# HGRN's cross products and head outputs regrouped by pairs and heads, and its softplus and scans spread over weight pieces

## The reference, cut to what matters

```python
    z = to_heads(f_logit.astype(f32), HGRN_HEADS)
    logf = jnp.logaddexp(jnp.log(lbh), jnp.log1p(-lbh) + jax.nn.log_sigmoid(z))
    k = -jnp.expm1(logf)
...
        b = jnp.cumsum(lfc, axis=-2)
        decay = jnp.exp(jnp.where(causal, b[..., :, None, :] - b[..., None, :, :], -jnp.inf))
        scores = jnp.einsum('bhtd,bhsd,bhtsd->bhts', qc, kc, decay)
        o = (jnp.einsum('bhts,bhsv->bhtv', scores, vc)
             + jnp.einsum('bhtd,bhdv->bhtv', qc * jnp.exp(b), state))
```

## Time and profile before

| | us |
|---|---|
| median of three runs | 2527.34 (2526.04 to 2527.4) |
| the profiled execution | 2526.51 |
| its span | 2524.4 |
| PE busy | 2417.4 (96%) |
| DVE busy | 1203.8 (48%) |
| ACT busy | 827.8 (33%) |
| POOL busy | 339.0 (13%) |
| mean granted TensorE clock | 0.979 |

### The profile page before, as it was taken

How to read it: one execution, slowest core, us unless ns; L and a number is a source line. 1 busy time by engine, 2 the same in 40 slices (tenths; PEclk the granted TensorE clock), 3 DMA queues, 4 the chain that set the end, 5 groups by cost and what they waited for, 6 DMA issues and landing times.

```text
span 2524.4 us, 32917 instructions
## 1 busy us (share of the span) xinstructions
PE 2417.4 (96%) x13323; PEld 2086.4 (83%) x13323; DVE 1203.8 (48%) x1449; ACT 827.8 (33%) x1178; POOL 339.0 (13%) x230
## 2 busy tenths in 40 slices
PE   5999999999999899999999999999898989999998
PEld 5888889788789798888898888898677979888887
DVE  5333336485546354323354333365895635533333
ACT  3221224332444343222233222242344434322221
POOL 2122112000003012000122100120032301210010
PEclk8999999999899999999999999999899999999998
DMA  4332332211223123333323333223221212332321
GB/s 146 93 100 92 93 99 76 92 59 50 64 72 96 39 76 92 100 96 96 100 68 92 100 100 100 94 66 95 88 77 52 90 35 76 92 100 92 101 94 40
DMA packets 169289, 213.44 MB, mean 85 GB/s; under 512 B 12840, under 2 KB 120776, under 8 KB 169160
## 3 DMA queue, kind: packets, MB, share of 16 engines
q1 hardware_dynamic: 169160, 211.62, 26.6%
HBM read 209.47 MB, written 2.10 MB: 84 GB/s over the span
## 4 chain that ended last, share of the span: by engine, by line
PE 85%; DVE 11%; ACT 2%; issue 1%; POOL 1%; DMA 0%; DVEq 0%; ACTq 0%
PE ps L1451 25%; PE ps L1453 25%; PE ps L1452 25%; DVE conv L1129 3%; DVE h L1012 2%; PE ps L1545 1%; DVE xlo L965 1%; PE ps L1941 1%; PE ps L1952 1%; PE ps L1837 1%; DVE y L1005 1%; POOL y L537 1%; PE ps L1492 1%; DVE wlo L930 1%; PE ps L1485 1%
## 5 line engine op out<-in xcount | busy, mean ns | idle before, releaser
L1451 PE MATMUL ps<-xlo,whi 128*128 128x512 f32 (+1 forms) x2472 | 892.4, 361 | 33.2 <-DVE xlo L965 14.7
L1453 PE MATMUL ps<-xhi,whi 128*128 128x512 f32 (+1 forms) x2472 | 886.7, 359 | 0.0
L1452 PE MATMUL ps<-xhi,wlo 128*128 128x512 f32 (+1 forms) x2472 | 886.5, 359 | 0.0
L930 DVE TENSOR_TENSOR wlo<-raw,whi 128x1024 fp32r<-128x1024 f32 x377 | 471.2, 1263 | 614.8 <-ACT whi L613 613.4
L613 ACT ACTIVATE whi<-raw 128x1024 fp32r<-128x1024 f32 x393 | 408.2, 1054 | 836.5 <-PE ps L1453 766.0
L1451 PEld LDWEIGHTS ps<-xlo,whi 128*128 128x128 f32 x2472 | 472.0, 191 | 103.7 <-issue 22.8
L1453 PEld LDWEIGHTS ps<-xhi,whi 128*128 128x128 f32 x2472 | 472.3, 191 | 67.0
L1452 PEld LDWEIGHTS ps<-xhi,wlo 128*128 128x128 f32 x2472 | 472.6, 191 | 66.1
L1451 PE MATMUL ps<-mid_lo,whi 128*128 128x512 f32 (+1 forms) x864 | 304.7, 353 | 0.0
L1453 PE MATMUL ps<-mid_hi,whi 128*128 128x512 f32 (+1 forms) x864 | 302.8, 350 | 0.0
L1452 PE MATMUL ps<-mid_hi,wlo 128*128 128x512 f32 (+1 forms) x864 | 301.1, 349 | 0.0
...
## 6 DMA issues: line engine op xcount, KB each, us to landing
...
```

The costliest lines, as they stand in the source:

```text
L930: v.tensor_tensor(flat(wlo[:, slot]), flat(raw[:, slot]), flat(whi[:, slot]).bitcast(f32), SUB).then_inc(lo_made, 1)
L1451: mm(out_ap, lh, rl, start=start, stop=False, skip_group_check=skip_group_check)
L1452: mm(out_ap, ll, rh, start=False, stop=False, skip_group_check=skip_group_check)
L1453: return mm(out_ap, lh, rh, start=False, stop=stop, skip_group_check=skip_group_check)
```

## The change

**Softplus and scans.** Abs, Exp and Ln no longer stand together behind a_f's sigmoid. They stand one by one behind ACT's first three splits of the next group (a_q). DVE forms `logf` behind its first split of the group after that (a_g), and runs the sixteen scans four at a time, one head behind each of that group's four splits.

**Cross products and heads.** The products are made in two halves of two heads, each half into three banks (0 to 2, then 3 to 5), and each half is copied by ACT in two copies. Only the second half waits for b_v to be moved out. `scores(0)` comes behind the products, then heads 0 and 1 (into banks 6 and 7), `scores(1)`, heads 2 and 3 (banks 4 and 5). ACT copies and squares head by head, with the exponents of steps 0 and 1 in between. The memory tokens' `m_hi` and `m_lo` (eight each) are made in two halves. `kd2` and `kd3` move to the place of `a_q`, and DVE makes the products and decayed keys ahead of its last three splits and of the wait for the b pieces.

**First kv piece.** It moves ahead of attention step 0; step 0 itself has none.

```diff
+CROSS_SLOT = [0, 2, 1, 3]
+O_BANK = [6, 7, 4, 5]
...
-    cross = place("cross", [P, 24, P], f32, y_at)
+    cross = place("cross", [P, 4, 8, P], f32, y_at)
...
-    kd2 = place("kd2", [P, 4, 2, P], f32, x_at + 2 * NB * FLOAT)
-    kd3 = place("kd3", [P, 4, P], f32, x_at + (2 * NB + 1024) * FLOAT)
+    kd2 = place("kd2", [P, 4, 2, P], f32, at(2 * NB))
+    kd3 = place("kd3", [P, 4, P], f32, at(2 * NB + 1024))
...
+        def softplus_step(n):
+            if n:
+                act.wait_ge(*softplus_last[0])
+            if n == 0:
+                E.run(a(soft[:], a_b[:], ACT.Abs))
+            elif n == 1:
+                E.run(a(soft[:], soft[:], ACT.Exp, scale=-1.0))
+            elif n == 2:
+                E.run(a(soft[:], soft[:], ACT.Ln, bias=ones[:, 0:1]), softplus_ready)
+            if n < 3:
+                softplus_last[0] = E.last
...
+            if first is not None:
+                first(exponents)
+            o0 = E.seen[o_ready.name]
             for i in range(n_steps + 2):
-                if i < n_steps:
-                    E.await_(negmax_ready)
-                    if i >= 2:
-                        act.wait_ge(probsT_ready, t0 + i - 1)
-                    nk = nk_of(i)
-                    for m in range(2):
-                        E.run(a(probs[:, i % 2, m, 0:nk], PS[:, 2 * (i % 2) + m, 0:nk], ACT.Exp,
-                                bias=negmax[:, i % 2, m:m + 1],
-                                accum_out=rowsum[:, i % 2, m:m + 1]), exp_done)
+                if i < n_steps and (first is None or i >= 2):
+                    exponents(i)
...
+                    if column_name(kind, g) == "a_q":
+                        softplus_step(kp)
...
                     if name == "a_f":
                         E.run(a(a_k[:], a_b[:], ACT.Sigmoid, scale=-1.0))
-                        E.run(a(soft[:], a_b[:], ACT.Abs))
-                        E.own()
-                        E.run(a(soft[:], soft[:], ACT.Exp, scale=-1.0))
-                        E.own()
-                        E.run(a(soft[:], soft[:], ACT.Ln, bias=ones[:, 0:1]), softplus_ready)
...
-                memory_input(l)
-                E.await_(cross_scores)
-                E.run(a(cross[:], blocks_of(2, 8), ACT.Copy), cross_copied)
-                E.await_(o_ready)
-                E.run(a(y[:, 0:4, :], PS[:, 4:8, :], ACT.Copy), o_copied)
-                E.own()
-                for k in range(4):
-                    square_into_ring(y[:, k, :])
+                def copy_cross(pair):
+                    E.await_(cross_scores)
+                    for n in range(2):
+                        E.run(a(cross[:, CROSS_SLOT[2 * pair + n], 0:6, :],
+                                blocks_of(3 * pair, 3 * pair + 3)[:, 6 * n:6 * n + 6, :], ACT.Copy), cross_copied)
+                def copy_o(hd):
+                    E.await_(o_ready)
+                    E.run(a(y[:, hd, :], PS[:, O_BANK[hd], :], ACT.Copy), o_copied)
+                    E.own()
+                    square_into_ring(y[:, hd, :])
+                def between_tiles(exponents):
+                    copy_cross(0)
+                    memory_input(l, range(0, 4))
+                    copy_cross(1)
+                    memory_input(l, range(4, KT))
+                    exponents(0)
+                    copy_o(0)
+                    copy_o(1)
+                    exponents(1)
+                    copy_o(2)
+                    copy_o(3)
...
+                    if name == "a_g":
+                        if kp == 0:
+                            E.await_(softplus_ready)
+                            E.run(v.scalar_tensor_tensor(out=logf[:], in0=a_b[:], scalar=0.0, in1=soft[:],
+                                                         op0=ALU.min, op1=SUB))
+                            logf_made = E.last
+                        dve.wait_ge(*logf_made)
+                        for t in range(TT):
+                            tok = slice(t * P, (t + 1) * P)
+                            E.run(v.tensor_tensor_scan(a_b[:, kp, tok], ones[:], logf[:, kp, tok], 0.0, MUL, ADD))
...
-                    if name == "a_f":
-                        E.await_(softplus_ready)
-                        E.run(v.scalar_tensor_tensor(out=logf[:], in0=a_b[:], scalar=0.0, in1=soft[:],
-                                                     op0=ALU.min, op1=SUB))
-                        E.own()
-                        for hd in range(4):
-                            for t in range(TT):
-                                tok = slice(t * P, (t + 1) * P)
-                                E.run(v.tensor_tensor_scan(a_b[:, hd, tok], ones[:], logf[:, hd, tok], 0.0, MUL, ADD))
...
-                done = split_to(done, 12 + LOOKAHEAD)
                 E.await_(decay_ready, 3)
                 E.run(v.tensor_tensor(lv[:, 0, :], lv[:, 0, :], flat(a_q[:]), MUL))
                 E.run(v.tensor_tensor(lv[:, 1, :], lv[:, 1, :], flat(a_k[:]), MUL))
                 E.own()
                 kd = lv[:, 1, :].rearrange("p (h t j) -> p h t j", t=TT, j=P)
-                E.piece += 4
-                E.group_done()
-                E.group += 1
                 for J in range(2):
                     E.run(v.tensor_tensor(kd2[:, :, J, :], kd[:, :, J, :],
                                           tile_decay[:, :, J + 1:J + 2].broadcast_to([P, 4, P]), MUL))
                 E.own()
                 E.run(v.tensor_tensor(kd3[:], kd2[:, :, 0, :], tile_decay[:, :, 2:3].broadcast_to([P, 4, P]), MUL),
                       cross_ready)
+                done = split_to(done, 12 + LOOKAHEAD)
+                E.piece += 4
+                E.group_done()
+                E.group += 1
...
+                    if i == 0:
+                        memory_lo(l, range(4, KT))
...
-                memory_lo(l)
+                memory_lo(l, range(0, 4))
...
-            scores(0)
             if first is not None:
-                first()
-            scores(1)
-            if first is not None:
-                E.await_(o_copied)
+                first(scores)
+                pe.wait_ge(o_copied, E.seen[o_copied.name] + 2)
+                kv_piece(kv_layer, E.piece, 0)
+                E.await_(o_copied, 4)
+            else:
+                scores(0)
+                scores(1)
...
-                if kv_layer is not None:
+                if kv_layer is not None and (first is None or i > 0):
                     kv_piece(kv_layer, E.piece, i)
...
-                for q in range(2):
-                    wait_banks(E.group + q)
+                assert b_bank == 4
+                wait_banks(E.group)
                 pe.wait_ge(level_merged, 2 * (len(LEVELS) + 1))
-                def between_tiles():
-                    E.await_(cross_ready)
+                def cross_products(pair):
                     kd = lv[:, 1, :].rearrange("p (h t j) -> p h t j", t=TT, j=P)
-                    for hd in range(4):
+                    for hd in (2 * pair, 2 * pair + 1):
                         for n, (i, j) in enumerate(CROSS):
                             key = kd[:, hd, j, :] if i - j == 1 else kd2[:, hd, j, :] if i - j == 2 else kd3[:, hd, :]
-                            last = mm(blocks_of(2, 8)[:, 6 * hd + n, :], key,
+                            last = mm(blocks_of(3 * pair, 3 * pair + 3)[:, 6 * (hd % 2) + n, :], key,
                                       lv[:, 0, hd * SEQ + i * P:hd * SEQ + (i + 1) * P], start=True, stop=True)
                     E.run(last, cross_scores)
-                    E.await_(cross_copied)
-                    for hd in range(4):
-                        for i in range(TT):
-                            terms = [(cross[:, 6 * hd + n, :], j) for n, (ii, j) in enumerate(CROSS) if ii == i]
-                            terms.append((scoresT[:, 4 * hd + i, :], i))
-                            for n, (s, j) in enumerate(terms):
-                                last = mm(PS[:, 4 + hd, i * P:(i + 1) * P], a_v[:, j, hd * P:(hd + 1) * P], s,
-                                          start=n == 0, stop=n == len(terms) - 1)
+                def head_output(hd):
+                    for i in range(TT):
+                        terms = [(cross[:, CROSS_SLOT[hd], n, :], j) for n, (ii, j) in enumerate(CROSS) if ii == i]
+                        terms.append((scoresT[:, 4 * hd + i, :], i))
+                        for n, (s, j) in enumerate(terms):
+                            last = mm(PS[:, O_BANK[hd], i * P:(i + 1) * P], a_v[:, j, hd * P:(hd + 1) * P], s,
+                                      start=n == 0, stop=n == len(terms) - 1)
                     E.run(last, o_ready)
+                def between_tiles(scores):
+                    E.await_(cross_ready)
+                    cross_products(0)
+                    wait_banks(E.group + 1)
+                    cross_products(1)
+                    E.await_(cross_copied, 2)
+                    scores(0)
+                    head_output(0)
```

(5 more changed lines are left out.)

24 lines of the change are left out of this document (17 added, 7 removed).

## The result

The changed kernel took 2507.72 us, the median of four executions (2506.52 to 2511.91; the longest is the profiled one); the kernel before, run beside it, took 2527.37. The ratio is 0.9922, with an interval of 0.9909 to 0.9935. The forecast was 2503.0 with a range of 2500 to 2507.5: the change is faster, as forecast, and the time lies 4.7 us above the forecast and 0.2 above the range. Later measurements repeated it: 14 executions have a mean of 2507.2 (2503.8 to 2511.9), against 2528.5 for 48 executions of the kernel before (2525.8 to 2530.8). So the gain is about 21.3 us, where 23.7 were forecast. The kernel before stands 1.2 us higher over its 48 executions than in the three that the forecast started from.

The account below looks back on a forecast made before the run. PE was taken to bound the kernel (85% of the chain). Gains of 6.2 (softplus) and 19.5 (cross products to spread) less 2.0 (clock) make 23.7 us, from 2526.51 to a median of about 2503, range 2500 to 2507.5.

Parts of the forecast that it names:

- Bound: Whole kernel: PE is 85% of the chain, so ACT or DVE changes gain only what they take from PE's waits.
- softplus: Group a_q: PE's 4.62 us pause and some 1.6 us of slow clock go; gain 6.2 us, bounds 4.6 and 6.3.
- DVE's order: Ahead of the cross products: DVE's `kd3` chain ends at about 598.1, 8 us before PE finishes the b pieces.
- ACT's copies: Cross products to step 0: ACT's copies are done before PE asks, with room of about 2 us.
- rival 3: Levels: DVE reaches them later and the softplus gain is given back; gain 17.5 us, time 2509, chance 0.03.
- rival 2: Heads and step 0: ACT's chain ends last instead of PE's; gain 17 to 19 us, time 2508.5, chance 0.12.
- PE's order: Last b piece to the column sums' end: PE's reordered work takes 24.5 us at full clock, the sums 3.6 of it.
- The way of `rstd`: Column sums to step 1's spread: 3.2 us through POOL, 2.35 covered by PE's work, so PE waits about 0.9.
- The clock behind the column sums: Spread and second kv piece: the clock falls with PE's pause of 0.9 us, costing 2 us, bounds 0 and 3.5.
- seams: Last b piece to step 1's spread: 0.3 us taken off the 19.8 us gain for seams between many short waits.
- Rival 1: Column sums: the clock holds through them; gain 25.7 us, time 2501, chance 0.25.
- The spread of executions: Whole kernel: the range allowed 0.7 us either way, from the runs shown.

Follow-up runs that it names:

- before_again: The kernel before, measured and profiled once more with no edit: mean 2527.9 us, ratio 0.9998.
- act_late: The changed kernel with ACT's eight `m_hi` all ahead of its copies of the cross products: mean 2507.8 us, ratio 0.9917 to the kernel before.
- wide: The changed kernel with step 0's 32 column-sum records made 128 columns wide instead of one: mean 2506.6 us, ratio 0.9912 to the kernel before.
- again: The changed kernel, measured and profiled once more with no edit: mean 2506.1 us, ratio 0.9912 to the kernel before.
- again2: The changed kernel, measured and profiled a third time with no edit: mean 2507.2 us, ratio 0.9915 to the kernel before.
- wide_split: The changed kernel with 128-column sums and half of the first kv piece on either side of them: mean 2501.1 us, ratio 0.9891 to the kernel before.
- wide_back: The changed kernel with 128-column sums and the first kv piece back in step 0, behind them: mean 2502.7 us, ratio 0.9894 to the kernel before.

## Why the prediction was right and wrong

**Bound, softplus, DVE's order, ACT's copies: right.** The softplus gained 6.35 us in A against a term of 6.2 (7.1 against `before_again`); the pause of the earlier trace rows is gone, `logf` doesn't wait, the levels give nothing back, and rival 3 with it is out. DVE's chain ends 8.4 us ahead of PE (8 forecast). ACT's copies are never waited for, and `act_late` shows that the margin was thin and real; rival 2 is out. PE's order at full clock was sized well too: from 601.8 to the start of the column sums it took 21.4 us, where the terms say 24.5 - 3.6 = 20.9.

**The way of `rstd`: the failed step in the touched part.** I took 3.3 us from the end of the sums to the spread (3.2 and 0.1), of which PE would wait 0.9. It took 4.3 us in all three profiles of the changed kernel and in `wide` (627.07 to 631.40, and 627.69 to 632.01). I had read POOL's operation where DVE stood idle beside it, 2.90 us, and the change itself put a weight split of DVE just ahead of it: 3.81 us, and 3.98 in `wide`. So the term lacks 1.0 us. The wait shows only in `wide` (1.95 us), where the clock holds. In the changed kernel the slow clock stretches PE's work ahead of the spread from 2.35 to 4.5 us, which fills the same time.

**The clock behind the column sums: right in kind, about right in size, wrong in place.** I let it fall with PE's pause, over the spread and a part of the kv piece, for 2 us with bounds of 0 to 3.5. It fell with no pause: at the end of the sums in this profile, further inside in `again` (whose sums took 4.58 us), and stayed down over the value product, `scores(3)`, the spread and most of the kv piece. What it cost is C, 6.2 us against 3.8, and what the sums took over their 3.68 at full clock: 2.6 us, and 2.7 in `again` and `again2`. The stretch between them cost next to nothing, since POOL would have held PE there anyway. In all, B + C is 35.7 us where my terms say 33.9 (27.8 to the spread, 0.3 for seams, 3.8 for the spread and the kv piece, 2 for the clock). The 1.8 are 1.0 for the way of `rstd`, 0.6 for the clock, 0.4 for PE's order and 0.1 for the sums at full clock, less the 0.3 for seams, which wasn't needed. Rival 1 (the clock holds) came in `wide_split` and `wide_back` alone, and there with the way of `rstd` covered as well.
The section of the Trainium skill that the prediction weighed ("TensorE: Matmul & The Clock Gate", section "Why this matters for your kernels") names idle gaps, and nothing else, as what lowers the clock in mid kernel. The trace disagrees: PE was busy for 21.30 of 21.30 and then 3.90 of 3.90 us, and the clock went from 1.00 to 0.50.

**The spread of executions: the other failed step, and the larger one.** The sum leaves the rest of the program as it was, and the range took 0.7 us either way from the three runs shown. The changed kernel's executions lie between 2503.8 and 2511.9. In the profiled execution the account is exact: against the first profile of before the touched part gained 22.0 us (23.7 forecast, 1.7 less), the rest of the program took 5.8 us more, and what comes ahead of a_f another 1.65 more; 22.0 - 5.8 - 1.65 = 14.6 us, the difference of the two spans. In `again2`, whose profiled execution took 2507.49, close to the median, the same three are 22.0 gained, 2.1 and 0.8 lost. (Against `before_again` the touched part gained 20.6, since there it took 1.4 less than in the first profile of before.) What decides where the clock falls in the rest I could not settle: the two profiles of before agree within 0.3 us and the three of the changed kernel differ by 7.6.

**The 4.7 us, and the bound.** Two slips of mine are in them. 2526.51 - 23.7 and the 0.8 to the median give 2503.6, not 2503, so 0.6 of the 4.7 is rounding. And the terms that I gave for the upper bound (1.5 + 1.6 + 1) give 2507.1 from 2503, or 2507.7 from 2503.6, not 2507.5. Of the other 4.1 us, 1.7 are the touched part and some 2.4 the rest. That last part is chance more than loss: over all executions the gain is 21.3 us, which the touched part alone gives (20.6 to 22.0), so no lasting loss outside it is seen. The three runs of before that I started from were low by 1.2, and the first four of the changed kernel were high by 0.5. That the median fell 0.2 us outside the range is luck of the same kind: the mean of the 14, 2507.2, lies within it, though near its end.
